# Input projection of a decoder layer: 14 column groups of 512 and one of 256 instead of 16 of 464

## The reference, cut to what matters

```
h = rms_norm(x, mix_norm_w)        # 2048 x 1024
z = h @ w_in                       # w_in: 1024 x 7424, z: 2048 x 7424
sq, sk, sv, rq, rk, rv, rg, mq, zg = split_cols(z, IN_SIZES)
```

## Time and profile before

| what | value |
|---|---|
| median of three runs | 5605.09 us |
| the profiled execution: from its first to its last instruction | 5600.4 us |
| TensorE busy | 5200.6 us, 93% of that span |
| first matmul of the projection starts | 71.92 us |
| last matmul of the projection starts | 1367.22 us |
| matmuls in the projection | 6144 (16 groups x 16 tiles x 24) |
| granted TensorE clock in the projection | full but for its first 3.7 us |

### The profile page before, as it was taken

The page is one execution under the profiler, slowest core; times in us unless marked ns, Lnnn a source line. Parts: engine busy times, 40 slices in busy tenths (PEclk is TensorE's granted clock), DMA queues, the critical chain, the costliest instruction groups (busy, mean ns, idle before and its releaser), DMA issues.

```text
span 5600.4 us, 88876 instructions
## 1 busy us (share of the span) xinstructions
PE 5200.6 (93%) x24906; PEld 4371.7 (78%) x24907; DVE 2741.4 (49%) x5402; ACT 1934.0 (35%) x3754; POOL 679.8 (12%) x767
## 2 busy tenths in 40 slices
PE   7999999998687799896999999999999999999996
PEld 6888888887566678685887878778877787888885
DVE  3000000000699744354566565775666666665564
ACT  3111111111355522222344444553444434343333
POOL 0000000000344300022011111111111111110110
PEclk7999999999799899897999999999999999999998
DMA  3221222122223243443467465764666656554556
GB/s 112 75 75 59 75 75 73 61 75 79 109 99 120 99 170 136 159 142 117 151 191 231 154 195 164 232 223 157 196 208 190 216 169 192 158 170 154 162 167 196
DMA packets 387048, 810.15 MB, mean 145 GB/s; under 512 B 62259, under 2 KB 113715, under 8 KB 380724
## 3 DMA queue, kind: packets, MB, share of 16 engines
q1 hardware_dynamic: 361188, 722.92, 37.5%
q0 software_dynamic: 25808, 86.59, 6.7%
HBM read 662.47 MB, written 155.26 MB: 146 GB/s over the span
## 4 chain that ended last, share of the span: by engine, by line
PE 46%; DMA 2%; DVE 2%; issue 1%; ACT 1%; DVEq 0%; SPq 0%; ACTq 0%; POOL 0%; POOLq 0%
PE e_acc L253 15%; PE e_acc L255 14%; PE e_acc L254 14%; DMA e_raw<-in_w_down 2%; PE e_xT L2049 1%; PE e_aT L2058 1%; DVE e_hid L2009 1%; ACT e_whi L1913 0%; DVE e_wlo L1974 0%; SPq L1806 0%; DVE e_alo L1984 0%; DVE e_glu L2011 0%; DMA e_xg<-h,e_rec_in 0%; ACT e_sg L1948 0%; DVE e_glu L2016 0%
## 5 line engine op out<-in xcount | busy, mean ns | idle before, releaser
L1974 DVE TENSOR_TENSOR e_wlo<-e_raw,e_whi 128x512 fp32r<-128x512 f32 x1544 | 953.1, 687 | 210.5 <-ACT e_whi L1913 207.7
L253 PE MATMUL e_acc<-e_whi,e_xhi 128*128 128x512 f32 x2592 | 1031.7, 398 | 17.8 <-issue 15.0
L255 PE MATMUL e_acc<-e_whi,e_xlo 128*128 128x512 f32 x2592 | 1012.9, 391 | 0.0
L254 PE MATMUL e_acc<-e_wlo,e_xhi 128*128 128x512 f32 x2592 | 1011.7, 390 | 0.0
L1913 ACT CAST e_whi<-e_raw 128x512 fp32r<-128x512 f32 x1544 | 830.9, 619 | 124.7 <-issue 84.7
L253 PE MATMUL p_acc<-p_hi,hT_hi 128*128 128x464 f32 x2048 | 765.8, 374 | 14.2 <-DVE p_lo L348 14.2
L255 PE MATMUL p_acc<-p_hi,hT_lo 128*128 128x464 f32 x2048 | 764.5, 373 | 0.0
L254 PE MATMUL p_acc<-p_lo,hT_hi 128*128 128x464 f32 x2048 | 761.7, 372 | 0.0
L348 DVE TENSOR_TENSOR p_lo<-p_raw,p_hi 128x464 fp32r<-128x464 f32 x128 | 79.5, 642 | 1078.9 <-ACT p_hi L318 1078.4
L253 PEld LDWEIGHTS e_acc<-e_whi,e_xhi 128*128 128x128 f32 x2592 | 487.2, 188 | 125.3 <-issue 27.9
L255 PEld LDWEIGHTS e_acc<-e_whi,e_xlo 128*128 128x128 f32 x2592 | 487.1, 188 | 103.1
(11 more groups left out here) (284 smaller groups left out, 6575.8 us busy)
## 6 DMA issues: line engine op xcount, KB each, us to landing
e_raw<-in_w_up SPq DMA_DIRECT2D x1032, 256.0 KB, 5.1
e_raw<-in_w_down SPq DMA_DIRECT2D x512, 256.0 KB, 6.7
z<-p_z SPq DMA_DIRECT2D x256, 232.0 KB, 2.0
e_bias<-in_b_up SPq DMA_DIRECT2D x129, 256.0 KB, 5.6
p_raw<-in_w_in SPq DMA_DIRECT2D x128, 232.0 KB, 2.8
b_gates<-z SPq DMA_DIRECT2D x16, 1536.0 KB, 7.1
oT<-x_oT SPq DMA_DIRECT2D x16, 1024.0 KB, 3.9
b_raw<-oT SPq DMA_DIRECT2D x16, 1024.0 KB, 9.4
```

What stands on the lines that cost most here:

```text
L253: pe.matmul(out, x_hi(k), w_hi(k), start=first, stop=False)
L254: pe.matmul(out, x_hi(k), w_lo(k), start=False, stop=False)
L255: mm = pe.matmul(out, x_lo(k), w_hi(k), start=False, stop=last)
L1974: dve.tensor_tensor(w_lo[s % 2][:, k, :], raw[:, k, :], w_hi[s % 2][:, k, :].bitcast(F32), ALU.subtract).then_inc(lo_made.sem, 1)
```

## The change

G becomes 512. That gives 14 whole groups, and the remaining 256 columns (`REST`) form a 15th. The last whole groups and the rest are written out behind the loops, so that the branches go away. The output tiles are cut from four to two. The order of the work on each queue is the same: loads and splits of the next group ahead of stores and copies of the present one.

```diff
-    GROUPS = 16
-    G = ZW // GROUPS
-    RAW, BANKS, OUTS = 4, 8, 4
+    G = 512
+    GROUPS = ZW // G
+    REST = ZW - GROUPS * G
+    RAW, BANKS, OUTS = 4, 8, 2
...
+            for k in range(KD):
+                load(GROUPS - 1, k)
+            store(GROUPS - 2)
+            for k in range(KD):
+                load(GROUPS, k, REST)
+            store(GROUPS - 1)
+            store(GROUPS, REST)
...
+            split(GROUPS - 1, 1)
+            evict(GROUPS - 2)
+            split(GROUPS, 0, REST)
+            evict(GROUPS - 1)
+            evict(GROUPS, REST)
...
+            def group(g, b, n=G):
+                pe.wait_ge(lo_made.sem, lo_made.after(g))
+                for i in range(TILES):
+
+                    pe.wait_ge(copied.sem, copied.after(g, i + 1 - BANKS))
+                    rows = slice(i * P, (i + 1) * P)
+                    three_pass(pe, acc[i % BANKS][:, 0:n],
+                               lambda k: hT_hi[:, k, rows], lambda k: hT_lo[:, k, rows],
+                               lambda k: w_hi[b][:, k, 0:n], lambda k: w_lo[b][:, k, 0:n],
+                               range(KD)).then_inc(summed.sem, 1)
+
             with pe.Fori(0, GROUPS // 2) as p:
                 for b in range(2):
...
+                    group(2 * p + b, b)
+            group(GROUPS, 0, REST)
```

More of the change, by code:

```diff
@@ L279, in _, with load, store @@
         def _(sp):
-            def load(g, k):
+            def load(g, k, n=G):
                 sp.wait_ge(lo_made.sem, lo_made.after(g, k + 1 - RAW))
-                sp.dma_start(raw[k % RAW][:], io["w_in"][k * P:(k + 1) * P, ds(g * G, G)]).then_inc(
+                sp.dma_start(raw[k % RAW][:, 0:n], io["w_in"][k * P:(k + 1) * P, ds(g * G, n)]).then_inc(
                     raw_in[k % RAW].sem, 16)
+            def store(g, n=G):
+                for i in range(TILES):
+                    sp.wait_ge(copied.sem, copied.after(g, i + 1))
+                    sp.dma_start(io["z"][i * P:(i + 1) * P, ds(g * G, n)],
+                                 zs[i % OUTS][:, 0:n]).then_inc(z_out[i % OUTS].sem, 16)
             for z in z_out:
@@ L289, in _ @@
                 load(0, k)
-            with sp.Fori(0, GROUPS // 2) as p:
+            with sp.Fori(0, GROUPS // 2 - 1) as p:
                 for b in range(2):
                     g = 2 * p + b
[L294 to L306, removed]
+                    for k in range(KD):
+                        load(g + 1, k)
+                    store(g)
+            for k in range(KD):
+                load(GROUPS - 1, k)
+            store(GROUPS - 2)
+            for k in range(KD):
+                load(GROUPS, k, REST)
+            store(GROUPS - 1)
+            store(GROUPS, REST)
             for z in z_out:
-                sp.wait_ge(z.sem, z.after(GROUPS - 1))
+                sp.wait_ge(z.sem, z.after(GROUPS))
         @blk.scalar
@@ L312, in _, with split, evict @@
             copied.open(act)
[L314 to L322, removed]
+            def split(g, b, n=G):
+                for k in range(KD):
+                    act.wait_ge(raw_in[k % RAW].sem, raw_in[k % RAW].after(g, 16 * (k // RAW + 1)))
+                    act.wait_ge(summed.sem, summed.after(g - 2))
+                    act.copy(w_hi[b][:, k, 0:n], raw[k % RAW][:, 0:n]).then_inc(hi_made.sem, 1)
+            def evict(g, n=G):
+                for i in range(TILES):
+                    act.wait_ge(summed.sem, summed.after(g, i + 1))
+                    j = 16 * (i // OUTS)
+                    act.wait_ge(z_out[i % OUTS].sem, z_out[i % OUTS].after(g, j))
+                    act.copy(zs[i % OUTS][:, 0:n], acc[i % BANKS][:, 0:n]).then_inc(copied.sem, 1)
+            split(0, 0)
+            with act.Fori(0, GROUPS // 2 - 1) as p:
                 for b in range(2):
                     g = 2 * p + b
[L326 to L340, removed]
+                    split(g + 1, 1 - b)
+                    evict(g)
+            split(GROUPS - 1, 1)
[3 more added lines that the diff above has]
+            evict(GROUPS, REST)
         @blk.vector
@@ L344, in _, with split @@
             lo_made.open(dve)
[L346 to L353, removed]
-                for b in range(2):
[L355 to L363, removed]
+            def split(g, b, n=G):
+                for k in range(KD):
+                    dve.wait_ge(hi_made.sem, hi_made.after(g, k + 1))
+                    dve.tensor_tensor(w_lo[b][:, k, 0:n], raw[k % RAW][:, 0:n], w_hi[b][:, k, 0:n].bitcast(F32),
+                                      ALU.subtract).then_inc(lo_made.sem, 1)
+            split(0, 0)
+            with dve.Fori(0, GROUPS // 2 - 1) as p:
+                for b in range(2):
+                    split(2 * p + b + 1, 1 - b)
+            split(GROUPS - 1, 1)
+            split(GROUPS, 0, REST)
         @blk.tensor
```

## The result

The median of four runs is 5575.12 us (5571.32 to 5575.94), against 5605.77 for the kernel before (5603.74 to 5606.97, four runs by then): ratio 0.9945, 95% interval 0.9931 to 0.9959, so 23 to 39 us faster. In a later comparison five runs gave 5571.77 against 5605.45, ratio 0.9942 (0.9929 to 0.9956). The forecast was 5583.4 with a range of 5574 to 5594: the sign and the range hold, and the time lies near the range's lower end, by the number of rival A (5577).

A forecast was written before the change was run, and what follows sets the result against it. The prediction took TensorE's matmul stream to bound the projection. TensorE -22.0 us, stage start +0.5 and end -0.2 gave -21.7 us, from 5605.1 to 5583.4 us, range 5574 to 5594.

The forecast's parts named there:

- rival A: Projection: surplus belongs to each matmul, not its columns; 120 ns a 256-column matmul, change -27.8 us, 5577 us; chance 22%.
- TensorE's stream is the stage, and the distance between starts its price: Projection: TensorE's matmul spacing sets the stage's length; 226.8 ns at 512 columns, whole groups 1219.3 us.
- The 256-column matmul: Projection's last group: 136 ns a matmul, 52.3 us for 384; ends 112 and 188 ns give 43.0 and 72.2 us.
- the 49 us: Projection's last group: the forecast is wrong if it takes under 49 us or over 63.
- rival A's floor: Projection's last group at 112 ns a matmul: change -31.0 us, 5574 us, the range's lower end.
- the rule: Projection: matmul and weight load take turns reading, so time goes with all columns read, 0.354 ns a column.
- The half clock: Projection's start: ten matmuls cost 3.97 us instead of 2.1; at 512 columns nine, the same loss of 1.9 us.
- Start and end of the stage: Projection: larger first loads, roundings and subtractions add 0.5 us; the smaller last copy and store take off 0.2 us.
- Two output tiles, order of loads, straight code: nothing: Projection: fewer output tiles, the next group's loads and splits, and written-out groups each cost TensorE nothing.
- B: Projection's last group bound by its weight loads: 188 ns a matmul, 72.2 us, change -1.8, 5603 us; chance 6%.
- C: Projection's 512-column stream doesn't settle as operands jump between tiles: 232 ns a matmul, 6 us slower, 5611; chance 5%.
- D: Projection: number of matmuls doesn't matter, equal columns take equal time; 384 fewer save about nothing, 5604 us; chance 3%.

The follow-up runs named there:

- The sizes kernel: The changed kernel with ten groups of 480 columns, then one each of 496, 448, 432, 416, 384, 320 and 128, chunks 2048 bytes apart: one execution 5619.35 us.

## Why the prediction came out as it did

**TensorE's stream is the stage, and the distance between starts its price.** Right: 14 groups of 87.04 us are 1218.6 against 1219.3 worked out from the merge stage's rows. That the price carried over from another stage is in part luck. The prediction didn't ask where the chunks start, and a step of 2112 bytes or a shift by 128 would have given 231.7 or 232.4 ns. One reading is off, and changes nothing in the sum: only ScalarE's idle time ahead of its roundings is waiting for transfers; ahead of its copies it waits for TensorE, 4.51 us at the last one.

**The 256-column matmul.** This is the step that failed. Predicted 52.3 us, measured 46.1: -6.2 us, and under the 49 us that the prediction had named as a sign of being wrong. It put the whole change at -21.7 us, where the stage shows -28.8; the range held because it reached down to rival A's floor, not because the rule was right. I took two sizes 48 columns apart, read their different surplus as a law in all columns read, and prolonged it over 208 columns. The sizes kernel shows a floor with a dear band, and 464 in the band. My argument against rival A (464 should then show 206.8) was the fault: it took 464 for a normal size. A's number, 120 ns, was right, though not its statement that every matmul pays the same. Nor was only the size of the term off: with time by all columns read, a narrower load never makes a stream longer, and at 512 it did (230.0 against 226.7 ns).

The Trainium skill says that loading the next weights takes no read bandwidth from the running matmul ("TensorE: Matmul & The Clock Gate", section "Step-by-step: what each phase is for"). The prediction had read A's sum out of that. This case's traces agree poorly with it: at 256 columns half the load made the stream faster, 113.4 against 120.0 ns, so there the load does cost the stream something. Whether that is read bandwidth no run shows.

**What was saved.** A matmul of 464 columns paid 3.9 ns over the floor: 6144 x 3.9 = 24 us. The 384 matmuls that are gone carried 13.3 ns each, 5.1 us. Together 29.1, and TensorE's sum went from 1295.5 to 1266.5 us (73.23 to 1339.64 plus one distance). So one sixth of the gain is the smaller number of matmuls, and five sixths are size and place together; the forecast had it as one rule.

Size and place can't be told apart within the 24 us, because neither brings much alone. From load to load the stage is 2.3 us shorter than before with 464 columns at the better place (1368.74 - 60.97 = 1307.8), 2.7 us shorter with 512 columns at the old step (1368.38 - 61.02 = 1307.4), and 28.8 us with both. By the matmul, the place is worth 0.6 ns at 464 and 5.0 at 512. "The old step" means that each chunk starts 64 bytes further against a multiple of 256: 1856 = 7 x 256 + 64, and 2112 = 8 x 256 + 64.

**The half clock.** Nine matmuls in 3.9 us [compare rows 2], and group 0 took 88.94 us, 1.9 over the others, as worked out. In the later run of the same kernel the stretch lasted 6.3 us and group 0 took 90.08: this term moves by a microsecond from run to run.

**Start and end of the stage.** From first load to first matmul 11.6 us instead of 10.8: +0.8, where I took +0.5. From the last matmul's start to the next stage's load 3.35 us instead of 4.02: -0.7, where I took -0.2.

**Two output tiles, order of loads, straight code: nothing.** Right. The first was measured alone. For the second, no wait of TensorE stands in the projection behind its first matmul. For the third, the group after the loop averages 120.0 ns over its 383 distances, the surplus that 320 and 416 columns have too, so fetching new code didn't show.

**The rivals.** B (188 ns) is out by the 120.0; of the sizes that were run, only 128 columns are slower than their streaming by much more than the floor, and that these 111.5 ns are the load's is read from the earlier trace rows, not tried. C didn't happen with chunks 2048 bytes apart. Its price, 231.7 ns against the 232 of the earlier trace rows, appears with chunks 2112 bytes apart, but by the place and not by jumps from tile to tile as C had it. D is out by the result.

**What stays open.** The stage accounts for 28.8 us, the medians for 30.7 and 33.7, the profiled spans for 26.2. These lie in one interval, and no run looked for the rest. Why the band from 432 to 496 is dear isn't settled; "blocks of 32 or 64" was tried and fails. Nor is it settled why the place within 256 bytes counts, and whether the band would lie elsewhere at another place: the sizes other than 512, 464 and 256 were run at one place only.

## What to carry to other kernels

Where a stage is a dense stream of matmuls, read the distance between two starts, subtract columns / clock, and ask of the remainder by size before trusting a rule through two points that lie close together. For three-pass float32r matmuls with a load each, 512 columns with chunks 2048 bytes apart cost the least per column here, and 432 to 496 were a bad choice. Change size and place one at a time and together: here each alone took under 3 us off the stage, and both 28.8. A narrow remainder down to 256 columns costs the same 13.3 ns; put first it shortened the wait for the first weights, and the stage by some 2.5 us.

## What the runs showed of the hardware

- The place of the moving operand in SBUF (or its distance from the stationary one, which was never moved) changes a matmul's time at full clock: 226.7 ns with a shift of 0 or 256 bytes, 228.9 with 64, 232.4 with 128, for the same 512 columns.
- A size can be dearer than its neighbours on both sides: 13.3 ns over streaming at 416 and at 512, 16.7 at 464 to 496.
- A smaller weight load can make a stream slower: 230.0 and 231.7 ns with 64 and 32 loaded columns against 226.7 with 128, at 512; faster only at 256 (113.4 against 120.0).
- At half clock none of this shows. The distances are streaming alone: 387 ns for 464 columns, 427 for 512 with the chunks unshifted, shifted by 128 bytes or loaded 64 columns wide, and 213 to 214 for 256.
